# A two-layer block in float32 on one core: where the second layer's modulation is computed

## The reference, cut to what matters

```
def modulation(cond, w, b):
    m = jax.nn.silu(cond) @ w + b
    return jnp.split(m, 3, axis=-1)
...
for l in range(DEPTH):
    sh, sc, gt = modulation(c, ada_w[l], ada_b[l])
    shc, scc, gtc = modulation(c_ctx, ada_w[l], ada_b[l])
    h = rms_norm(x, norm_pre[l]) * (1.0 + sc[:, None]) + sh[:, None]
    hc = rms_norm(xc, norm_pre[l]) * (1.0 + scc) + shc
    z = h @ w_in[l]
    ...
    out = merge_branches(z, (y_a, y_b, y_c), w_branch[l], w_out[l])
    x_new = x + gt[:, None] * rms_norm(out, norm_post[l])
```

## Time and profile before

| | us |
|---|---|
| median of 3 runs | 2042.17 |
| lowest and highest run | 2038.86, 2043.2 |
| the profiled execution, its own time | 2040.52 |
| span of the profile | 2038.7 |
| PE busy | 1959.7 |
| DVE busy | 1300.0 |
| ACT busy | 979.4 |
| POOL busy | 38.7 |

### The profile page before, as it was taken

How to read it: one execution, slowest core, us unless ns; L and a number is a source line. 1 busy time by engine, 2 the same in 40 slices (tenths; PEclk the granted TensorE clock), 3 DMA queues, 4 the chain that set the end, 5 groups by cost and what they waited for, 6 DMA issues and landing times.

```text
span 2038.7 us, 29542 instructions
## 1 busy us (share of the span) xinstructions
PE 1959.7 (96%) x12560; PEld 1705.0 (84%) x12560; DVE 1300.0 (64%) x1748; ACT 979.4 (48%) x1459; POOL 38.7 (2%) x23
## 2 busy tenths in 40 slices
PE   6999999999999999999899999999999999989998
PEld 3789999899898899999878887688888888768887
DVE  3987656788645878865565566665556555676555
ACT  2355445465334546544454445654445444565444
POOL 2400000000000000000000000000000000000000
PEclk8999999999999999999999999999999999999999
DMA  8544555434676543455445554355555555425554
GB/s 327 206 133 140 170 181 168 140 125 145 215 250 226 188 135 129 141 194 182 149 145 188 188 171 155 114 176 186 186 176 183 188 186 187 165 74 174 186 187 143
DMA packets 95410, 351.84 MB, mean 173 GB/s; under 512 B 10608, under 2 KB 10736, under 8 KB 94768
## 3 DMA queue, kind: packets, MB, share of 16 engines
q1 hardware_dynamic: 94320, 343.70, 50.1%
q0 software_dynamic: 672, 4.75, 0.6%
q10 hardware_dynamic: 288, 1.51, 0.2%
HBM read 348.87 MB, written 1.05 MB: 172 GB/s over the span
## 4 chain that ended last, share of the span: by engine, by line
PE 84%; DVE 11%; ACT 3%; DMA 2%; issue 1%; SPq 0%; DVEq 0%; ACTq 0%
PE PS L578 25%; PE PS L580 25%; PE PS L579 25%; DVE w_lo L1867 3%; DMA raw<-weights 2%; ACT w_hi L1344 1%; PE PS L656 1%; PE PS L761 1%; PE PS L994 1%; PE PS L780 1%; PE PS L1076 1%; PE PS L957 1%; PE PS L846 1%; PE PS L770 0%; PE PS L1087 0%
## 5 line engine op out<-in xcount | busy, mean ns | idle before, releaser
L1867 DVE TENSOR_TENSOR w_lo<-raw,w_hi 128x1024 fp32r<-128x1024 f32 x600 | 740.1, 1243 | 401.6 <-ACT w_hi L1344 400.2
L1344 ACT ACTIVATE w_hi<-raw 128x1024 fp32r<-128x1024 f32 x600 | 624.4, 1055 | 390.2 <-DMA raw<-weights 385.9
L578 PE MATMUL PS<-h_hi,w_hi 128*128 128x256 f32 x1568 | 455.6, 291 | 12.5 <-DVE h_lo L1885 4.7
L579 PE MATMUL PS<-h_lo,w_hi 128*128 128x256 f32 x1568 | 444.9, 284 | 0.0
L580 PE MATMUL PS<-h_hi,w_lo 128*128 128x256 f32 x1568 | 444.7, 284 | 0.0
L578 PE MATMUL PS<-w_hi,h_hi 128*128 128x512 f32 (+1 forms) x1024 | 391.2, 382 | 9.8 <-DVE h_lo L2242 6.5
L580 PE MATMUL PS<-w_hi,h_lo 128*128 128x512 f32 (+1 forms) x1024 | 382.4, 373 | 0.0
L579 PE MATMUL PS<-w_lo,h_hi 128*128 128x512 f32 (+1 forms) x1024 | 381.5, 373 | 0.0
L578 PEld LDWEIGHTS PS<-h_hi,w_hi 128*128 128x128 f32 x1568 | 301.6, 192 | 29.9 <-issue 19.9
L579 PEld LDWEIGHTS PS<-h_lo,w_hi 128*128 128x128 f32 x1568 | 302.1, 193 | 1.3 <-issue 1.2
L580 PEld LDWEIGHTS PS<-h_hi,w_lo 128*128 128x128 f32 x1568 | 302.0, 193 | 0.0
(11 more groups left out here) (259 smaller groups left out, 1859.5 us busy)
## 6 DMA issues: line engine op xcount, KB each, us to landing
raw<-weights SPq DMA_DIRECT2D x638, 512.0 KB, 3.3
x<-weights SPq DMA_DIRECT2D x6, 512.0 KB, 10.6
layer<-weights SPq DMA_DIRECT2D x3, 512.0 KB, 10.2
layer<-layer_in SPq DMA_DIRECT2D x1, 1536.0 KB, 6.7
layer<-layer_in POOLq DMA_DIRECT2D x1, 1536.0 KB, 6.9
cx<-ctx_in POOLq DMA_DIRECT2D x1, 1024.0 KB, 8.5
x<-x_in SPq DMA_DIRECT2D x1, 1024.0 KB, 7.0
out<-arena SPq DMA_DIRECT2D x4, 256.0 KB, 2.1
```

The source lines that it names most:

```text
L578: pe.matmul(dst, hi, m_hi_, start=first, stop=False, **kw)
L579: pe.matmul(dst, hi, m_lo_, start=False, stop=False, **kw)
L1344: nc.scalar.activation(w_hi[:, r, :], raw[:, r, :], ACT.Copy).then_inc(w_hi_ready, 1)
L1867: V.tensor_tensor(w_lo[:, r, :], raw[:, r, :], f32(w_hi[:, r, :]), ALU.subtract).then_inc(w_lo_ready, 1)
```

## The change

Layer 1's modulation no longer runs on PE nor through the ring. The host lays `ada_w[1]` out transposed: 24 pieces of 128 output columns (partitions) by 1024 inputs (free dimension). A new input `cond_in` holds both conditions, copied to all 128 partitions. In passes 0 and 1, when PE has finished the inverse transform of the long convolution (`conv_done`), POOL loads `cond_in` (1 MB) into `q`, which is free by then, and the first two pieces (512 KB each) into halves of `k` and `v`. ACT applies Silu to the condition rows in place, just ahead of the merge. In each of the 12 rounds of these two merges DVE runs `ada_row`: two operations, one for each condition, each of which multiplies a piece with the condition row and writes the sum along the row to one column of `ada_sums`. It stands between the splits and the wait for `sel`. POOL loads piece n once the row of piece n - 2 is done. Pass 1's merge has three slots a round, like the others, and 36 slots instead of 60 go through the ring there. `mod_vectors(1)` reads `ada_sums` instead of `mod_raw`.

```diff
-    stretch("pass1", dram_pass[0], MERGE_AT)
-    stretch("pass1_merge", None, MERGE_SLOTS + ADA_SLOTS)
-    stretch("pass1_wo", dram_pass[0] + MERGE_AT + MERGE_SLOTS, 8)
+    stretch("pass1", dram_pass[0], PASS_SLOTS)
...
+        cond_rows = q[:, :, :].rearrange("p (w k) t -> p w (k t)", w=2)
+        ada_w = [k[:, 0:4, :].rearrange("p k t -> p (k t)"), v[:, 0:2, :].rearrange("p a c -> p (a c)")]
+        ada_prod = scratch(4608, SLOT)
...
@@ GpSimd
+            def load_ada(n):
+                pool.dma_start(ada_w[n % 2], weights[dram_pass[1] - ADA_SLOTS + n]).then_inc(ada_w_loaded[n % 2], 16)
+
+            def modulation_rows(p):
+                first, end = ADA_ENDS[p], ADA_ENDS[p + 1]
+                pool.wait_ge(conv_done, p + 1)
+                pool.dma_start(cond_rows, cond_in).then_inc(cond_loaded, 16)
+                load_ada(first)
+                load_ada(first + 1)
+                for n in range(first + 2, end):
+                    pool.wait_ge(ada_sum, 2 * (n - 1))
+                    load_ada(n)
+
+            modulation_rows(0)
+            modulation_rows(1)
             pool.wait_ge(src_ready, 16)
@@ TensorE
-                each = 5 if p == 1 else 3
                 for i in range(4):
                     for b in range(3):
-                        c = start[f"pass{p}_merge"] + each * (3 * i + b)
-                        if p == 1:
-                            ada(c, b, 0, i)
-                            c += 1
+                        c = start[f"pass{p}_merge"] + 3 * (3 * i + b)
...
-                        if p == 1:
-                            ada(c + 1, b, 1, i)
-                            c += 1
                         pair(c + 1, 2 * b + 1)
-                    if p == 1:
-                        ada_turn(ADA_TURNS + i, 7)
@@ ScalarE
+                if p < 2:
+                    act.wait_ge(cond_loaded, 16 * (p + 1))
+                    nc.scalar.activation(cond_rows, cond_rows, ACT.Silu).then_inc(cond_rows_act, 1)
@@ VectorE
+            def ada_row(n):
+                if n in ADA_ENDS:
+                    dve.wait_ge(cond_rows_act, ADA_ENDS.index(n) + 1)
+                dve.wait_ge(ada_w_loaded[n % 2], 16 * (n // 2 + 1))
+                for w in range(2):
+                    i = 2 * n + w
+                    if i >= 1:
+                        dve.wait_ge(ada_sum, i)
+                    V.scalar_tensor_tensor(ada_prod, ada_w[n % 2], 1.0, cond_rows[:, w, :], ALU.mult, ALU.mult,
+                                           accum_out=ada_sums[:, i:i + 1]).then_inc(ada_sum, 1)
...
-                        for j in range(-1, each - 1):
+                        for j in range(-1, 2):
                             split(c + j + AHEAD)
-                            if p == 1 and j == 2:
-                                ada_piece(c + 1, ADA_TURNS + i, b, (6, 7))
+                        if p < 2:
+                            ada_row(ADA_ENDS[p] + 3 * i + b)
                         dve.wait_ge(sel_ready, i * 3 + (12 * p + b + 1))
...
-                    if p == 1:
-                        ada_take(ADA_TURNS + i, 7)
+                if p < 2:
+                    dve.wait_ge(ada_sum, 2 * ADA_ENDS[p + 1])
```

More of the change, by code:

```diff
@@ L58 @@
 ADA_BUFS = RING + 2
+ADA_ENDS = [0, 12, ADA_SLOTS]
 ADA_EARLY = ADA_SLOTS - ADA_TURN
@@ L119, in build @@
     dram = dram_pass[1] + PASS_SLOTS
-    for p in (0, 2):
+    for p in range(3):
         start[f"pass{p}_merge"] = start[f"pass{p}"] + MERGE_AT
@@ L305, in build @@
         ada_used = sem("ada_used")
+        cond_loaded = sem("cond_loaded")
+        cond_rows_act = sem("cond_rows_act")
+        ada_w_loaded = [sem(f"ada_w_loaded{j}") for j in range(2)]
+        ada_sum = sem("ada_sum")
         raw_loaded = [sem(f"raw_loaded{r}") for r in range(RING)]
@@ L420, in build @@
         block = ctx.enter_context(nc.Block())
[L422 to L429, removed]
         def f32(ap):
@@ L504, in _ @@
             for n0, d0, count in stretches:
[L505 to L515, removed]
                 for j in range(count):
@@ L658, in ada_half @@
                 return mm
[L660 to L671, removed]
             def ada_turn(turn, bank):
@@ L676, in ada_turn @@
                 for j in range(6):
-                    mm = pe.matmul(PS[:, bank, 2 * j:2 * j + 2], ada_rows_of[turn // ADA_TURNS][:, j * P:(j + 1) * P],
+                    mm = pe.matmul(PS[:, bank, 2 * j:2 * j + 2], ada_rows[:, j * P:(j + 1) * P],
                                    col("ada_sum", 0, 2), start=True, stop=True)
@@ L1532, in run_pass @@
                 gates("gc", 2)
-                each = 5 if p == 1 else 3
+                if p < 2:
+                    act.wait_ge(cond_loaded, 16 * (p + 1))
+                    nc.scalar.activation(cond_rows, cond_rows, ACT.Silu).then_inc(cond_rows_act, 1)
                 for i in range(4):
                     for b in range(3):
-                        c = start[f"pass{p}_merge"] + each * (3 * i + b)
-                        for j in range(-1, each - 1):
+                        c = start[f"pass{p}_merge"] + 3 * (3 * i + b)
+                        for j in range(-1, 2):
                             split(c + j + AHEAD)
                         act.wait_ge(merge_free, i * 3 + (15 * p + b + 1))
-                        act.wait_ge(w_used, c + each)
+                        act.wait_ge(w_used, c + 3)
                         nc.scalar.activation(sel[:, b, :], PS[:, 2 * b + 1, :], ACT.Sigmoid).then_inc(sel_ready, 1)
@@ L1913, in post_norm_pairs, with ada_piece @@
                 return take
[L1915 to L1920, removed]
+            def ada_piece(turn, m, banks):
+                dve.wait_ge(ada_used, ADA_TURN * turn + 2 * m + 2)
                 if m == 0 and turn > 0:
                     dve.wait_ge(ada_turned, turn)
[L1923 removed]
+                V.tensor_copy(ada_rows[:, m * T:(m + 1) * T], PS[:, banks[m % 2], 0:T]).then_inc(ada_rows_ready, 1)
             def ada_take(turn, bank):
                 dve.wait_ge(ada_turned, turn + 1)
[L1927 to L1928 removed]
+                V.tensor_copy(mod_raw[:, 12 * turn:12 * turn + 12], PS[:, bank, 0:12]).then_inc(ada_taken, 1)
             def modulation(turn, m):
[L1931 removed]
+                ada_piece(turn, m, (0, 1))
             def mod_part(l, turns_, first, end):
[L1934 to L1935 removed]
+                if l == 0:
+                    dve.wait_ge(ada_taken, turns_)
+                else:
+                    dve.wait_ge(ada_sum, 2 * ADA_SLOTS)
+                m = [mod_raw, ada_sums][l][:, :].rearrange("p (f w) -> p f w", w=2)
                 for w in range(2):
@@ L2720, in pack @@
     for l in range(DEPTH):
-        token(g["ada_w"][l])
+        if l == 0:
+            token(g["ada_w"][l])
+        else:
+            for c in range(0, 3 * D, P):
+                slots.append(g["ada_w"][l][:, c:c + P].T)
         w = g["w_in"][l]
```

17 lines of the change are left out of this document (9 added, 8 removed).

## The result

The changed kernel took 2023.0 us at the median of four runs (2016.2 to 2025.8) against 2042.7 (2038.9 to 2043.3) for the kernel before: a ratio of 0.990, 95% interval 0.989 to 0.992. Measured in two further sets, each beside the kernel before, it took 2019.7 and 2018.9, with ratios of 0.989 (0.987 to 0.990) and 0.990 (0.988 to 0.992). By the medians the gain is 19.7, 22.0 and 22.2 us, some 21. The forecast was 2020.0 in a range of 2016.8 to 2028.

The account below looks back on a forecast made before the run. PE, busy 96% of the span, was taken as the bound. 2040.5 - 21.7 + 0.2 = 2019.0 us from the profiled execution, 2020.7 from the median; forecast 2020.0, range 2016.8 to 2028 (2016.8 to 2023.5 for the forecast case alone).

Parts of the forecast that it names:

- The removal: Pass 1's merge on PE: without modulation slots and turns it shrinks to pass 0's length, -21.7 us.
- The price of a pair: Two row operations with sums on DVE each round: 2.8 us, bounded by 2.46 below and 3.2 above.
- Cost in the rounds: Row operations in DVE's gap before the product, merges of passes 0 and 1: PE loses 0 at either bound.
- The 2.1 us in hand: How much later DVE may be in every merge round before PE waits for the next round's first split.
- The sign that I gave with it: On DVE in the merges: at most 0.5 us idle before the product, not growing over the rounds.
- The ends: End of both changed merges, where PE waits for last product, sum and split: 0.1 each, +0.2 us, range 0 to 0.8.
- Silu: ACT's Silu on 128x2048 ahead of both merges: 1.91 us, delays the first split but fits with 1.7 to spare, cost 0.
- The loads: POOL's loads beside the ring loads in the merges: ring loads land in about 4 to 5 us; cost 0, up to +1.
- the limit without a stall: Longest landing of a ring load in the merges before PE stalls: 4.1 + 2.1 = 6.2 us.
- Late loads: Rival, 0.12: POOL's pieces slow ring loads to 7 us, delaying the third split; +13 over 20 rounds, 2032.
- Half rate: Rival, 0.07: row operations run at half rate, a pair takes 5.0 us and DVE becomes the bound; 2053.
- No effect: Rival, 0.04: pass 1's modulation was hidden on PE anyway, so the time stays at 2040.

Follow-up runs that it names:

- the removal alone: The changed kernel without the loads of conditions and pieces, Silu and the row operations, second layer's modulation left out; 2021.1 us, ratio 0.990.
- the four operations: The changed kernel with each condition's row operation done twice, four in each round of both merges; 2041.0 us, ratio 1.000.

## Why the prediction was right

- **The removal, -21.7.** Right in the merge (21.72 in the first profiles, 130.96 - 108.66 = 22.30 in the second), and by the removal alone in the end time (ratio 0.990 on the same chip as 0.989 for the whole change). That the first pair agrees to the hundredth is luck. Taking an undisturbed twin of the stretch as a template worked better than adding up the removed instructions, which gave 21.9.
- **The price of a pair, 2.8.** It is 2.49: 1.22 an operation and 0.08 for the sum. I had priced the sum at 0.165, by the smallest DVE operation; it is half of that. The lower bound was 2.46. The 0.1 that the upper bound put between the two operations came from no row; the second one starts 0.03 behind the read of the first.
- **Cost in the rounds, 0.** Right to 0.5 us (0, 0.3 and 0.5 in three profiles), and the experiments say how far: one more operation still costs nothing in the rounds, two more make DVE the bound, and the same pair in another place costs 0.23 a round. The 2.1 us in hand was good to 0.2. The sign that I gave with it was not: DVE idles up to 2.3 us before a product, not 0.5 at most, since I had read the gap from one round and the rounds differ. DVE's own round was over-sized, 5.06 for 4.5, so the point from which DVE decides is 4.2 us of rows, not 3.6.
- **The ends, +0.2.** 0.0 in the first profile: the waits for the split sum are 0.73 and 0.84 as before.
- **Silu, 0.** It takes 1.91 us, at 229.49 to 231.40, and the split behind it is in time; PE does not wait in the round.
- **The loads.** POOL's first three loads, at 202.8, landed in 5.1, 5.8 and 8.8 us. The ring loads of the merge landed in 4.2 us at the median, 6.8 at the most; I had said 4 to 5, and 6.2 for the limit without a stall. The slowest is above that limit and caused no stall in that profile; loads of 7.2 and 7.1 us in pass 1's merge of the two others go with the waits of 0.3 and 0.5. The limit was put too low: the chain behind it counted every operation of DVE by its duration, and back to back they follow each other faster. Here the prediction was right with less to spare than it said.
- **Late loads, 12%.** The mechanism is there (2.9 to 3.9 us as the longest wait for one split) and reaches PE in single rounds of two of the three profiles, for 0.5 us at the most, not for 13.
- **Half rate, 7%.** Refuted: 1.22 us for 1024 elements with a sum is the rate of a two-input operation. The Trainium skill's sentence (Vector Engine (DVE) Microarchitecture Reference, Points that are easy to get wrong), read as half the rate of a plain product, does not hold for this form here. The price that it would have had was over-sized too: pairs of twice the length, as the four operations are, cost 21 us and not the 34 that I gave it, so its end time would have been 2041, no change rather than slower.
- **No effect, 4%.** Refuted: pass 1's merge is 21.7 shorter, with the removal alone too.
- **The rest.** PE's busy time fell by 19.4 in the first profiles, not 21 to 22; matmuls of 256 columns follow each other at 0.21 us at half clock (around 642 us in the first profile) and at 0.12 at full, and PE is busy 1940.3, 1938.1 and 1935.7 us in three profiles of the changed kernel, 1959.7 and 1958.7 in two of the kernel before. DVE's rose by 49.6, not 61: 48 x 1.22 is 58.6, the sums are 3.8 more, the removed copies are 5.7. Of the remaining 7, 5.5 are overlap: each read is recorded as starting 0.07 us before its operation ends, and each pair 0.08 before the last split ends.
- **The median.** 2023.0 and not 2020.0: the first four executions lie between 2016 and 2026 and their mean granted clocks between 0.982 and 0.986, the shorter the higher; two further sets gave 2019.7 and 2018.9. The range for the forecast alone, 2016.8 to 2023.5, does not follow from its sentence: 3.3 below and 1.0 above 2020.0 is 2016.7 to 2021.0. The 2023.0 lies above that, and is within 2023.5 by a margin for which no row was named.

## What to carry to other kernels

In this kernel, work on an engine off the critical path was free only in a certain place: look for the wait on which the engine idles each round, put the work right ahead of that wait, and compute what the bounding engine needs next from it and when. Put behind that wait instead of ahead of it, the same 2.5 us a round cost 10 us in the two merges here. And when the engine's capacity is the question, count back-to-back pitches of its operations, not their durations, and average over rounds that differ.

## What the runs showed of the hardware that I had not expected

- Reading DVE's accumulator takes 0.08 us, against ACT's 0.19, and a product of two float32 rows with its sum runs at the rate of the plain product: 1.22 us for 128x1024.
- The granted clock of TensorE is lost in equal portions. In all eleven profiles every drop up to 2010 us cost 1.7 us or two or three times that, near a stretch in which PE had waited or had ended its work, but not behind every such wait and not in every execution of the same kernel. The sums differ between two executions of one kernel by up to 7 us (34.1, 30.7 and 27.2 for the changed kernel), and explain most of the difference between runs: span less this sum is 1989.7, 1987.2 and 1987.8.
- Two queues that load at once do not slow each other evenly. With POOL's loads the median landing of a ring load in the changed kernel's merges was 3.5 to 4.3 us, and single ones went to 6.1 to 7.2. Without them the slowest took 5.1 and 4.1. The median does not tell the two apart: with the removal alone it was 3.3 and 4.2.
